# Attention in a two-block transformer kernel: values as TensorE's stationary operand, two heads in the two column halves, and the softmax division moved behind the product

## The reference

```python
s = jnp.einsum('brhnqd,brhnkd->brhnqk', qs, kb) * (D ** -0.5)      # first kind, one of three dilated branches
e = jnp.exp(s - m)
l = jnp.sum(e, axis=-1, keepdims=True)
o = jnp.einsum('brhnqk,brhnkd->brhnqd', e, vb) / l
...
s = jnp.where(valid[:, :, None, :], s, -jnp.inf)                    # second kind, on the keys that an index picked
p = jax.nn.softmax(s, axis=-1)
o = jnp.einsum('bqhk,bqkhd->bqhd', p, vg.astype(jnp.float32))
```

## Time and profile before

| | |
|---|---|
| median of 3 runs | 2943.47 us (2941.57 to 2943.89) |
| the profiled execution's own time | 2941.83 us |
| its span | 2940.0 us |
| PE busy, share of the span | 2802.6 us, 95% |
| PE weight loads, DVE, ACT, GpSimd busy | 2235.2, 1202.5, 1129.4, 1223.6 us |
| mean granted clock of TensorE | 0.972 |
| chain that ended last: share on PE | 79% |
| attention product L2048, 640 records | 89.7 us busy |

### The profile page before, as it was taken

How to read it: one execution, slowest core, us unless ns; L and a number is a source line. 1 busy time by engine, 2 the same in 40 slices (tenths; PEclk the granted TensorE clock), 3 DMA queues, 4 the chain that set the end, 5 groups by cost and what they waited for, 6 DMA issues and landing times.

```text
span 2940.0 us, 44118 instructions
## 1 busy us (share of the span) xinstructions
PE 2802.6 (95%) x15368; PEld 2235.2 (76%) x15368; DVE 1202.5 (41%) x2246; ACT 1129.4 (38%) x1950; POOL 1223.6 (42%) x630
## 2 busy tenths in 40 slices
PE   9998999999999989999999889999999998999997
PEld 7777777888877777888888567778788666778776
DVE  4555455551256553655403774410113685410012
ACT  4454244443335533444423326432323325432331
POOL 3313135554432222355544451364553451264553
PEclk9999999999999989999999999999999999899998
DMA  3211012223221101222232120122222120122222
GB/s 128 73 50 37 9 65 92 93 93 101 92 82 58 58 9 37 72 93 94 99 105 76 58 72 30 55 94 95 93 93 74 58 79 30 43 92 95 93 93 93
DMA packets 62874, 217.25 MB, mean 74 GB/s; under 512 B 6576, under 2 KB 6704, under 8 KB 62480
## 3 DMA queue, kind: packets, MB, share of 16 engines
q1 hardware_dynamic: 62416, 214.28, 22.3%
q0 software_dynamic: 320, 1.12, 0.2%
HBM read 213.28 MB, written 2.10 MB: 73 GB/s over the span
## 4 chain that ended last, share of the span: by engine, by line
PE 79%; DVE 8%; ACT 4%; POOL 4%; issue 3%; DVEq 1%; ACTq 0%; POOLq 0%
PE bank L1819 51%; POOL wL L742 4%; PE bank L2139 3%; PE bank L1868 2%; PE bank L1846 2%; PE bank L2048 2%; PE bank L1996 2%; PE bank L1997 2%; PE bank L1998 2%; ACT wH L912 2%; PE bank L2037 1%; PE bank L2025 1%; PE bank L1876 1%; DVE bias L1696 1%; PE bank L1935 1%
## 5 line engine op out<-in xcount | busy, mean ns | idle before, releaser
L742 POOL TENSOR_TENSOR wL<-raw,wH 128x1024 fp32r<-128x1024 f32 x380 | 920.8, 2423 | 1255.2 <-ACT wH L912 1254.9
L1819 PE MATMUL bank<-hH,wH 128*128 128x512 f32 x1744 | 722.4, 414 | 30.4 <-POOL wL L742 17.1
L1819 PE MATMUL bank<-hL,wH 128*128 128x512 f32 x1744 | 686.0, 393 | 0.0
L1819 PE MATMUL bank<-hH,wL 128*128 128x512 f32 x1744 | 684.8, 393 | 0.0
L912 ACT ACTIVATE wH<-raw 128x1024 fp32r<-128x1024 f32 x380 | 399.5, 1051 | 264.0 <-PE bank L1819 236.1
L1819 PEld LDWEIGHTS bank<-hH,wH 128*128 128x128 f32 x1744 | 330.7, 190 | 151.8 <-issue 57.9
L1819 PEld LDWEIGHTS bank<-hH,wL 128*128 128x128 f32 x1744 | 331.3, 190 | 71.3 <-issue 10.3
L1819 PEld LDWEIGHTS bank<-hL,wH 128*128 128x128 f32 x1744 | 330.3, 189 | 71.9
L1819 PE MATMUL bank<-hidH,wH 128*128 128x512 f32 x864 | 337.6, 391 | 2.4 <-POOL wL L742 2.4
L1819 PE MATMUL bank<-hidH,wL 128*128 128x512 f32 x864 | 336.2, 389 | 0.0
L1819 PE MATMUL bank<-hidL,wH 128*128 128x512 f32 x864 | 336.2, 389 | 0.0
(11 more groups left out here) (328 smaller groups left out, 3871.0 us busy)
## 6 DMA issues: line engine op xcount, KB each, us to landing
raw<-w_dram SPq DMA_DIRECT2D x398, 512.0 KB, 3.3
x<-x_dram SPq DMA_DIRECT2D x4, 512.0 KB, 9.4
out_dram<-x SPq DMA_DIRECT2D x1, 2048.0 KB, 6.2
const<-const_dram SPq DMA_DIRECT2D x1, 1229.0 KB, 14.1
par_next<-par_dram POOLq DMA_DIRECT2D x5, 168.0 KB, 2.6
qkT<-pos_dram POOLq DMA_DIRECT2D x1, 256.0 KB, 7.1
const<-const_dram SPq DMA_DIRECT2D x1, 131.0 KB, 2.2
```

The costliest lines, as they stand in the source:

```text
L742: pool.tensor_tensor(wL[:, s, :], raw[:, s, :], wH[:, s, :].bitcast(F32), ALU.subtract).then_inc(w_lo.sem, 1)
L1819: mm = pe.matmul((out or ACC[bk])[:, :], wt[:, s, c:c + P], rhs, start=first and k == 0 and j == 0, stop=last and k == tiles - 1 and j == 2)
```

## The change

- The product is turned: weights are the 64 columns of `v` of a head, the 128 query columns of the transposed probabilities stream. Head 0 writes partitions 0 to 63 of `TRO`, head 1 partitions 64 to 127, so one bank holds the finished layout and the transposes of `ao` go away. Both heads are done together, in odd slots from 3 on: pair p = (n - 3)//2, **ahead of** that slot's transposes of step n - 1.
- The sum can no longer scale a row on the way out, since tokens are columns now. PE spreads each reciprocal column over 64 partitions by a product with the identity, into `OA` (one matmul per head).
- In flush slots ACT copies the whole of `OA` (128x512) to `ao`, and DVE multiplies `TRO` by it in place of its copy. The 32 reads of `OA` per layer go away.
- PE's first product of the next query tile (slots 11, 19, 27) waits for both.

```diff
 ACT, attention(w, n)
                     if m >= 2:
-                        act.wait_ge(pv_done.sem, pv_done.at(w, m - 1))
+                        act.wait_ge(pv_done.sem, pv_done.at(w, m - m % 2))
...
-                m = n - 2
-                if 0 <= m < 32:
-                    c, p = m % 4, m // 2
-                    act.wait_ge(pv_done.sem, pv_done.at(w, m + 1))
-                    act.wait_ge(rsum.sem, rsum.at(w, m + 1))
-                    if p >= 2:
-                        act.wait_ge(tro_done.sem, tro_done.at(w, p - 1))
-                    act.activation(ao[:, p % 2, m % 2 * HD:m % 2 * HD + HD], OA[:, 0:HD], ACT.Copy,
-                                   scale=st[:, RS + c:RS + c + 1]).then_inc(oa_read.sem, 1)
+                if n % 8 == 2 and n >= 10:
+                    f = (n - 10) // 8
+                    act.wait_ge(sum_spread.sem, sum_spread.at(w, f + 1))
+                    if f:
+                        act.wait_ge(piece_ready.sem, piece_ready.at(w, n0 + f))
+                    act.activation(ao, OA[:, :], ACT.Copy).then_inc(sum_copied.sem, 1)
 DVE, attention(w, n)
                 if n % 8 == 2 and n >= 10:
                     f = (n - 10) // 8
-                    dve.wait_ge(tro_done.sem, tro_done.at(w, 4 * f + 4))
+                    dve.wait_ge(pv_done.sem, pv_done.at(w, 8 * f + 8))
+                    dve.wait_ge(sum_copied.sem, sum_copied.at(w, f + 1))
...
-                    dve.tensor_copy(att_piece(w.b, f), TRO[:, :]).then_inc(piece_ready.sem, 1)
+                    dve.tensor_tensor(att_piece(w.b, f), TRO[:, :], ao, ALU.mult).then_inc(piece_ready.sem, 1)
 PE, attention(w, n, fill)
                 for i in fill[0:1]:
                     half_step(w, i // 4, i % 4, 0)
+                if n >= 3 and n % 2:
+                    p = (n - 3) // 2
+                    f, i, _ = att_step(2 * p)
+                    pe.wait_ge(pt_copied.sem, pt_copied.at(w, 2 * p + 2))
+                    pe.wait_ge(rsum.sem, rsum.at(w, 2 * p + 2))
+                    if p % 4 == 0 and p >= 4:
+                        pe.wait_ge(piece_ready.sem, piece_ready.at(w, n0 + p // 4))
+                        pe.wait_ge(sum_copied.sem, sum_copied.at(w, p // 4))
+                    for j in range(i + 1):
+                        for h in range(2):
+                            mm = pe.matmul(TRO[h * HD:h * HD + HD, f * P:f * P + P],
+                                           v[:, j, (2 * f + h) * HD:(2 * f + h) * HD + HD],
+                                           pt[:, h, j * P:j * P + P], start=j == 0, stop=j == i)
+                    mm.then_inc(pv_done.sem, 2)
+                    for h in range(2):
+                        c = RS + (2 * p + h) % 4
+                        mm = pe.matmul(OA[h * HD:h * HD + HD, f * P:f * P + P], st[:, c:c + 1].broadcast_to([P, HD]),
+                                       ident, start=True, stop=True)
+                    if p % 4 == 3:
+                        mm.then_inc(sum_spread.sem, 1)
                 m = n - 1
...
-                m = n - 2
-                if 0 <= m < 32:
-                    f, i, h = att_step(m)
-                    pe.wait_ge(pt_copied.sem, pt_copied.at(w, m + 1))
-                    if m:
-                        pe.wait_ge(oa_read.sem, oa_read.at(w, m))
-                    for j in range(i + 1):
-                        mm = pe.matmul(OA[:, 0:HD], pt[:, m % 2, j * P:j * P + P],
-                                       v[:, j, (2 * f + h) * HD:(2 * f + h) * HD + HD], start=j == 0, stop=j == i)
-                    mm.then_inc(pv_done.sem, 1)
-                if n >= 4 and n % 2 == 0:
-                    p = (n - 4) // 2
-                    pe.wait_ge(oa_read.sem, oa_read.at(w, 2 * p + 2))
-                    if p % 4 == 0 and p >= 4:
-                        pe.wait_ge(piece_ready.sem, piece_ready.at(w, n0 + p // 4))
-                    pe.transpose(TRO[:, p % 4 * P:p % 4 * P + P], ao[:, p % 2, :], ident).then_inc(tro_done.sem, 1)
```

More of the change, by code:

```diff
@@ L392, in build @@
             pt2 = sb("pt2", [P, 2, S], F32, share)
-            ao2 = sb("ao2", [P, 2, P], F32, share)
+            ao2 = sb("ao2", [P, S], F32, share)
             st2 = sb("st2", [P, 17], F32, share)
@@ L469, in build @@
         pv_done = signal("pv_done", 32, 32)
-        oa_read = signal("oa_read", 32, 32)
-        tro_done = signal("tro_done", 16, 16)
+        sum_spread = signal("sum_spread", 4, 4)
+        sum_copied = signal("sum_copied", 4, 4)
         conv_in = signal("conv_in", 12, 0)
@@ L555, in tile4 @@
             return gv[:, a + 4 * t:a + 4 * t + 4]
-        ao1 = eb[1][:, 0:2, :]
-        ATT = ((qT1, kT1, v1, sc1, pt1, ao1, st1, 0, N_ATT1), (qT2, kT2, v2, sc2, pt2, ao2, st2, 4, N_ATT2))
+        ao1 = eb[1][:, :, :].rearrange("p h c -> p (h c)")
+        ATT = ((qT1, kT1, v1, sc1, pt1, ao1, st1, 0, N_ATT1), (qT2, kT2, v2, sc2, pt2, ao2[:, :], st2, 4, N_ATT2))
         MN, SUM, RS = 0, 4, 8
@@ L991, in attention @@
             def attention(w, n):
-                q, k, v, sc, pt, ao, st, _, _ = ATT[w.b]
+                q, k, v, sc, pt, ao, st, _, n0 = ATT[w.b]
                 if n < 32:
```

## The result

| | before | after |
|---|---|---|
| median, same chip | 2942.52 us (2935.79 to 2943.89, 4 runs) | 2973.04 us (2968.21 to 2975.92, 4 runs) |
| profiled execution's own time, span | 2941.83, 2940.0 us | 2975.92, 2974.1 us |
| mean granted clock | 0.972 | 0.968 |

A forecast was written before the change was run, and what follows sets the result against it. TensorE, busy 95% of the span, was taken as the bound, with a cross-engine chain in the second kind from slot 16. Layers gave -0.4 + 10.4, the clock +4.1: +14.1 on 2941.8, 2956 us, range 2938 to 2980 (about 0.8).

The forecast's parts named there:

- Price (b): Turned product: both heads run at once in column halves, 0.217 us per pair step against 2 x 0.21 before.
- (c): Price of changing to the 64-column shape and back: 0.30 us per excursion, 0.15 where PE comes from a wait.
- halves that don't run densely: Rival on the column halves: 0.32 us per pair step gives 2979, chance 0.04; one after the other 3004, 0.02.
- First kind: Layers with float32r matmuls between slots: PE work -1.6 us, flush waits +1.4, so -0.2 per layer.
- Slots 3 to 15 of the second kind: Per second-kind layer: PE's pair work +0.8 us, and slot 11's wait for copy and multiplication +0.4.
- Odd slots: Second kind, slots 17 to 31: work that filled the wait moves behind the copy, 0.37 us each, +3.0 per layer.
- Flush slots 19 and 27: Second kind, no filler or slack: full 1.4 us wait for ACT's copy and DVE's multiplication twice, +2.8 per layer.
- the clock, 4.1 in all: Idle PE in slots 19 and 27 may drop the clock: four slots, 6 in 10 each, 1.7 us, +4.1.
- The tail: Second kind, slots 32 to 34: 6.45 us before becomes 4.0 to 5.3, -1.8 per layer.
- The clock staying low through slots 18 to 33: Rival: clock stays at 1.2 GHz there in the second kind, +49 us, 3005, or 2980 if it recovers; chance 0.12.
- hidden flush waits: Rival: flush waits are covered and the clock stays, 13.3 us fall out, 2943 us; chance 0.20.
- faster: Rival: TensorE's saving arrives with waits covered, -6.5 us per layer, 2916 (chance 0.04), or half, 2929 (0.08).

The follow-up runs named there:

- early: Changed kernel with ACT's copy of the spread sums and DVE's multiplication ahead of the flush slot's exponential and bias step: 2966.10 us, ratio 1.0068.
- swap: Changed kernel; second kind's even slots from 16: ACT copies `pt` before the exponential, PE's half step moves behind the transposes: 2965.03 us, ratio 1.0093.
- early_swap: Changed kernel with both reorderings, flush copy and multiplication early, and `pt` copy and transposes ahead: 2944.56 us, ratio 1.0009 to the kernel before.
- second_only: Kernel before with the new attention in the second kind of block alone: 2951.50 us, ratio 1.0043, span 2942.9.

## Why the prediction was right or wrong

The direction was right, and the range (2938 to 2980) held 2973.04; the size was not: +30.5 us against +14. That the range held is in part luck, since 13 of the us come from a norm that the sum did not contain. The steps that failed are the queueing behind DVE's new wait, put at nothing (+10.1 us measured in the first kind against -0.4), and the clock outside the changed lines, put at nothing (+13). Step by step:

- **Price (b), 0.217 us per pair step, and (c)**: right. 1.02 us for i = 2 as forecast. Where no wait interferes, the first kind's intervals between scores changed by +0.22, -0.21 to +0.02, -0.21 to -0.24 and -0.49 us for i = 0 to 3 (forecast +0.20, 0, -0.20, -0.41). The two cases of halves that don't run densely fall. The Trainium skill's load rule ("TensorE: Matmul & The Clock Gate", Part 3) would have made this product longer than the 0.217 us per pair step that the trace has, as the delta rule's rows already said.
- **First kind, -0.2 per layer**: this is the step that failed. The +1.4 of direct flush waits was right (0.50 us in slot 11 and 0.76 in slot 19); the term beside it was not. I wrote that DVE's convolution, queued behind the new wait, came 1 us later, "which should be covered". It does come 1.1 us later, but first in that queue stands the copy of the token sums, which PE needs at once. I had looked at one customer of DVE, not at the next instruction in its queue. PE's waits for these copies went from 0.8 us to 4.2 a layer (2.74 of them in slot 26), its idle time from the first scores to the last from 0.9 to 5.5, and the low clock that follows the longest wait adds to it. The score-to-score interval of slot 26 alone grew from 9.21 to 12.37 us in the first layer and to 13.67 in the second. +5.0 per layer, not -0.2; early gives nearly all of it back.
- **Slots 3 to 15 of the second kind, +0.8 and +0.4**: about right, +1.04 and +1.65 over the first eight intervals of the two layers.
- **Odd slots, +0.37 each**: right in kind, and at most 0.17 too much. Those clear of a flush grew by 0.35, 0.20 and 0.33 us (3.56 to 3.91, 4.03 to 4.23, 4.46 to 4.79), and swap, which only moves work into the wait, takes them below before.
- **Flush slots 19 and 27, 1.4 us each on top, and the clock, 4.1 in all**: right in kind and nearly in size. The two flush intervals of the last layer and the ones behind them grew by 2.21, 1.04, 3.04 and 0.49, together 6.8 us; the terms give 4 x 0.37 + 2.8 + 2.0 = 6.3. PE idled 2.17 us in slot 27, inside the 2.1 to 2.4 forecast, and 2.04 in slot 19, just below. The two parts, waits and clock, are not measured apart.
- **The tail, -1.8, with +0.37 for slot 31**: too small. From the last scores to the piece it went from 12.86 us (2501.07 to 2513.93) to 10.05 (2539.49 to 2549.54), -2.8, and up to the next norm -3.5 and -3.7; less of that stretch also runs at 1.2 GHz (6.8 us in place of 13.7 in the first of the two layers).

```profile
2545.49 0.63 PE L2055 MATMUL bank<-const,sc 128*128 128x128 f32 x4 [0.81 <-ACT pt L1005]
...
2546.80 1.09 PE L2038 MATMUL bank<-pt,v 128*64 128x128 f32 x16 [0.69 <-ACT pt L1005]
...
2548.85 0.69 DVE L1416 TENSOR_TENSOR piece<-bank,ao 128x512 f32<-128x512 f32 x1 [3.79 <-ACT ao L1011]
```

- **The clock elsewhere, forecast at nothing**: missing term, +13 us. I counted the clock only where the change makes PE wait. The kernel has norms that run either in 13.9 us or in 24 to 27 (three of the eight were caught so in one trace or another), and the first norm of all was caught both ways with no changed instruction ahead of it.
- **The clock staying low through slots 18 to 33** did not happen, and **hidden flush waits** and **faster** fall. That PE's saving arrives when the waits are covered is shown by early_swap's spans between scores in the second kind, from slot 16 on, where before had hardly any idle time to give; it is 1.8 and 1.6 us a layer (1.2 and 2.8 over all slots, but there the clock's dips in slots 0 to 3 differ by more than that), plus a tail that is 3.6 and 2.4 shorter, not 6.5 in the slots.

Open: what decides which way the norm goes (where the code of the loop falls among its transfers is untested), and so whether the change itself brings it. Shown is that a long one is a norm at 1.2 GHz, that at the turn between the second kind's layers it comes with a gap behind its first four products or with a clock already down, that unread matmuls ahead of it are no sure cure, and that it can strike before any changed code. It also stays open why second_only's span grew by only 2.9 us where its two layers' stretches give 9.7; the traces put the rest in short stretches of full clock where before had 1.2 GHz.

## What to carry to other kernels

When an edit puts a wait into an engine's queue, follow that queue instruction by instruction and ask of each who needs it: the bottleneck engine's next product hung on a small copy two places behind the new wait, and the first kind lost 10.1 us, most of it there, where the second kind with all that was forecast for it lost 10.9. Turning a product so that 64-column weights work in both column halves does save matmul time, but here the time only arrived when the waits that the removed work used to cover were filled or removed, as swap and early did. And look in the trace for places that have two speeds before crediting or blaming an edit with some 13 us: compare stage by stage, and beside a pair of kernels in which that place behaves alike.

## What the runs showed of the hardware

- A fully busy PE can stay at 1.2 GHz. In the long norm of the changed kernel PE was busy 15.00 of 15 us (2284 to 2299) with the granted clock at 0.50, in steps of 3.41 us of four wide products and eight records of one column; the clock rose again only behind the norm, in wide matmuls (low for 30.7 us). The same steps take 1.83 us at full clock, and there it stayed at 1.00 (before, 2250 to 2263 us). In none of the fourteen traces did the clock, once down in a norm, come back before the norm's end.
- At the turn between the second kind's layers PE stands in up to two places for nothing that the profile names ("issue") or for ACT's first tile: 1.85 and 2.15 us in the changed kernel, 0.53 us and nothing in the kernel before, where the unread matmuls ran mostly at half clock and took 4.27 us instead of 2.40. In early they took 4.03 us, and the gaps were 0.57 and 1.85: slower idle work shortens the first, not the second. Both gaps end a steady time behind a 16 KB transfer of instructions (1.9 to 2.1 us and 1.2 to 1.5).
- Sixteen passes of 64-column weights in two column halves plus the spread of two reciprocals (i = 3) take 1.25 us (2537.66 to 2538.91), as the delta rule's rows had it by extrapolation from eight passes in one half.
